# Low-part scores of a differential attention as two 64-row matmuls, both maps of a chunk together

## The chip, the cores and the metric

One NeuronCore of a Trainium2 chip runs the whole program. The metric is the device time of one execution in microseconds (us), the median of several runs; lower is better. TensorE is the matmul engine (PE in the profile, its weight loads PEld), VectorE is DVE, ScalarE is ACT, GpSimd is POOL, and SyncE (SP) issues DMAs.

## The reference, cut to what matters

One layer of an encoder over 2048 prompt frames and 64 sample frames. A combined input projection feeds two branches; the change is in the first, differential attention with 4 heads. Every head has two maps (m = 0, 1) with 64-wide queries and keys of their own, and one 128-wide value:

```python
scores = einsum('bqhmd,bkhmd->bhmqk', q, k) * ATTN_SCALE      # m = 0, 1; d = 64
scores = where(visible, scores + bias, -inf)                  # ALiBi, chunks of 64
p = softmax(scores)
a = p[:, :, 0] - lam * p[:, :, 1]
out = einsum('bhqk,bkhe->bqhe', a, v)
```

The second branch is a gated recurrence in chunks; both are normalised, gated and projected back.

## The kernel before

The program goes through the four heads one after the other (head 0 written out, heads 1 to 3 in a loop), and in each through 17 query tiles `t`: 16 prompt tiles of 128 frames and the sample tile (`SAMPLE`, 64 frames). A prompt tile `t` sees 128 (t + 1) keys, the sample tile 192; `chunks_of(t)` cuts the keys into chunks of up to 512, 41 chunks per head, of which 28 are 512 wide, four each 384, 256 and 128 wide, and one 192 (the sample's).

Matmuls here run on values split into a high part (type f32r) and a low part, the difference. For the scores the split is along the array's rows: for each map, 64 rows hold the high part of the keys and 64 the low part, `kp[:, m, :]`. The queries of a map come twice: `q2[:, m, 0, :]` has the high part in both halves of the rows, `q2[:, m, 1, :]` the low part in both. So two 128-row matmuls per map and chunk, which add up in one PSUM bank (`qkb[:, u % 2]`), make high times (high + low) and low times (high + low): line 660. Map 0 uses bank 0, map 1 bank 1.

TensorE's program for tile `t` is `project(h, t, first)`: two halves, b = 1 (the recurrence's columns) and then b = 0 (the attention's), each of 8 steps `kt` of three 512-column matmuls (line 534: high x with high and low weights, low x with high weights). The scores of the tile before are laid between these steps: the units (chunk, map), in order, one behind each of the steps kt = 1 to 7 of b = 1 and one behind kt = 0 of b = 0 (lines 542 to 546). Ahead of kt = 2 of b = 0 come the recurrence's scores of the tile before (`rec_scores`, line 560, same two banks), ahead of kt = 6 three transposes. Behind the projection come `rec_output` (lines 575 to 577), `attend` (transposes of the attention weights, line 596, and their products with the values, line 605) and the transposes of this tile's queries and keys (`transpose_qk`, lines 636 to 646). In the sample tile the line 605 and line 577 matmuls have 64 rows in one block each; float32 matmuls show as two instructions.

`qk(h, t, c, m)` waits for its bank (`qk_free`, signalled by VectorE's read two uses ago), issues its two matmuls and signals `qk_done`. VectorE's `biased_scores` (line 1055) reads each bank, adds the bias, keeps the running maximum and frees the bank, in the order chunk 0 map 0, chunk 0 map 1, chunk 1 map 0, and so on; between chunk 0 and 1 it does `finish` of the tile before, behind chunk 1 `apply_decay`. Then ScalarE takes the exponentials (line 828), and VectorE combines the maps (line 1077).

The natural-order copies of queries and keys are made by ScalarE (high parts, lines 773 and 774) and VectorE (low parts, lines 1003 and 1004) in `qn`, and transposed by TensorE into `q2` and `kp`. Behind the last head an epilogue projects back (lines 687 to 700).

Of the kernel before, what the change touches and what calls it, by code (L numbers as in the profile page):

```python
# [25 lines left out]
P = 128  # L26
# [5 lines left out]
HD = 64  # L32
VD = 128
CHUNK = 64
KT = D_MODEL // P
PT = SEQ // P
NT = PT + 1
SAMPLE = NT - 1
# [25 lines left out]
def chunks_of(t):  # L64
    k0, n = keys_of(t)
    return [(k0 + c, min(512, n - c), c) for c in range(0, n, 512)]
# [26 lines left out]
def build(nc, x_prompt, x_sample, cache_k, cache_v, state_h, norm_g, w_in, lambda_qk, subln_g, rec_lb,  # L93
# [5 lines left out]
    with ctx:  # L99
        def sb(name, shape, dt=f32):  # L100
            return ctx.enter_context(nc.sbuf_tensor(name, shape, dt))
# [13 lines left out]
        kp = sb("kp", [P, 2, SLOTS * P], f32r)  # L115
# [2 lines left out]
        bias = sb("bias", [P, SEQ])  # L118
        at = sb("at", [P, 2, 512])
        qn = sb("qn", [P, 8, P], f32r)  # L120
        q2 = sb("q2", [P, 2, 2, P], f32r)
        kn = sb("kn", [P, 2, P])
        zz = sb("zz", [P, 2, P])
# [100 lines left out]
        def need(eng, h, name, n):  # L224

            eng.wait_ge(S[name], h * PER[name] + (PRIME.get(name, 0) + n))
# [261 lines left out]
        def _(pe):  # L488
# [19 lines left out]
            def project(h, t, first):  # L508

                units = qk_units(t - 1) if t > 0 else []
                slot = t % XRING
                if first:
                    pe.wait_ge(S["x_hi"], t + 1)
                    pe.wait_ge(S["x_lo"], t + 1)
                else:
                    pe.wait_ge(S[f"xr_in{slot}"], (h - 1) * (16 * XR_PER[slot]) + 16 * (t // XRING + 1))
                steps = [(b, kt) for b in (1, 0) for kt in range(KT)]
                for b, kt in steps:  # L520
                    if kt == 0:
                        need(pe, h, ("qk_split", "pb_free")[b], t)
                    if b == 0 and kt == 6:
                        transpose_recurrence(h, t, first)
                    if b == 0 and kt == 2 and t > 0:
                        rec_scores(h, t - 1)
                    if t == 0 and b == 1:
                        name, n = lo_of(kt)
                        need(pe, h, "w_hi_ready", kt + 1)
                        need(pe, h, name, n)  # L530
                    for part in range(2):
                        x = xr[:, slot, part, kt, :]
                        for w in ((w_hi, w_lo) if part == 0 else (w_hi,)):
                            last = mm(pab[:, b, :], x, w[:, kt, 512 * b:512 * b + 512],  # L534
                                      start=(kt == 0 and part == 0 and w is w_hi),
                                      stop=(kt == KT - 1 and part == 1))
                    if t == SAMPLE and b == 0 and kt < KT - 1:
                        last.then_inc(S["w_freed"], 1)
                    if b == 1 and kt >= 1:
                        if first and kt == (2 if t > 0 else KT - 1) and t < NT - 1:  # L540
                            x_transposes(t + 1)
                        for c, m in units[kt - 1:kt]:
                            qk(h, t - 1, c, m)
                    if b == 0 and kt == 0:
                        for c, m in units[KT - 1:]:
                            qk(h, t - 1, c, m)
                    if kt == KT - 1:
                        last.then_inc(S[("proj_done", "proj_b")[b]], 1)

# [30 lines left out]
            def attend(h, t, first):  # L580
                if t == SAMPLE:
                    need(pe, h, "cache_in", 48)
                need(pe, h, "fin_done", t)
                chunks = chunks_of(t)

                if first and t + 2 < NT:
                    pe.wait_ge(S["x_lo"], t + 3)

                def transposes(c):
                    u = t_use["at", t, c]  # L590
                    need(pe, h, "t_evac", u - 1)
                    apart(pe)
                    need(pe, h, "combined", at_index[t, c] + 1)
                    apart(pe)
                    for b, _, n in blocks_of(t, c):
                        last = tr(tb[0:n, u % 2, b:b + P], scores[:, 0, chunks[c][2] + b:chunks[c][2] + b + n],  # L596
                                  ident[:, :])
                    last.then_inc(S["at_t"], 1)

                def values(c):  # L600
                    u = t_use["at", t, c]
                    need(pe, h, "t_evac", u + 1)
                    blocks = blocks_of(t, c)
                    for j, (b, slot, n) in enumerate(blocks):
                        last = mm(oar[:, 0, 0:VD], at[0:n, u % 2, b:b + P], vv[0:n, slot, :],  # L605
                                  start=(c == 0 and j == 0), stop=(c == len(chunks) - 1 and j == len(blocks) - 1))
                    return last

                transposes(0)
                for c in range(len(chunks)):  # L610
                    if t == SAMPLE - 1 and c == 1:
                        transpose_qk(h, SAMPLE)
                    if c + 1 < len(chunks):
                        transposes(c + 1)
                    last = values(c)
                    if t == SAMPLE - 1 and c == 1:
                        for m in range(2):
                            qk(h, SAMPLE, 0, m)
                last.then_inc(S["pv_done"], 1)

            def transpose_recurrence(h, t, first):
# [24 lines left out]
                        last = tr(tb[:, u % 2, P * j:P * j + P], qn[:, 4 + j, :].bitcast(f32), ident[:, :])  # L646
                last.then_inc(S["k_t"], 1)

            def qk_units(t):
                return [(c, m) for c in range(len(chunks_of(t))) for m in range(2)]  # L650

            def qk(h, t, c, m):

                if c == 0:
                    need(pe, h, "t_evac", t_use["k", t] + 1)
                k0, w, _ = chunks_of(t)[c]
                u = qk_use["qk", t, c, m]
                need(pe, h, "qk_free", u - 1)
                for part in range(2):
                    last = mm(qkb[:, u % 2, 0:w], q2[:, m, part, :], kp[:, m, k0:k0 + w],  # L660
                              start=(part == 0), stop=(part == 1))
                last.then_inc(S["qk_done"], 1)

            def head(h, first):
                for t in range(NT):
# [54 lines left out]
        def _(act):  # L720
# [47 lines left out]
            def attention_columns(h, t):  # L768
                need(act, h, "proj_done", t + 1)
                pa = pab[:, 0, :]  # L770
                q_out = qn[:, 0:4, :].rearrange("p (m a) (d e) -> p m a d e", m=2, d=2)[:, :, 0]
                q_in = pa[:, 0:P].rearrange("p (m e) -> p m e", m=2).unsqueeze(2).to_broadcast([P, 2, 2, HD])
                F(q_out, q_in, ACT.Copy)
                F(qn[:, 4:6, 0:HD], pa[:, P:2 * P].rearrange("p (m e) -> p m e", m=2), ACT.Copy)
                need(act, h, f"k_out{t % 2}", 16 * (t // 2))
                F(kn[:, t % 2, :], pa[:, P:2 * P], ACT.Copy)
                if t == 0:
                    need(act, h, "v_out", 0)
                F(vv[:, slot_of(t), :], pa[:, 2 * P:3 * P], ACT.Copy)
                F(zz[:, 0, :], pa[:, 3 * P:4 * P], ACT.Copy)  # L780
                F(ez[:, 0, :], pa[:, 3 * P:4 * P], ACT.Exp, scale=-1.0).then_inc(S["a_evac"], 1)
# [122 lines left out]
        def _(dve):  # L904
# [58 lines left out]
            def link(h, ins):  # L963

                chain[0] += 1
                ins.then_inc(S["vec_chain"], 1)
                need(dve, h, "vec_chain", chain[0])
# [30 lines left out]
            def attention_columns(h, t):  # L998
                need(dve, h, "a_evac", t + 1)
                pa = pab[:, 0, :]  # L1000
                q_blocks = qn[:, 0:4, :].rearrange("p (m a) (d e) -> p m a d e", m=2, d=2)
                q_in = pa[:, 0:P].rearrange("p (m e) -> p m e", m=2).unsqueeze(2).to_broadcast([P, 2, 2, HD])
                tt(q_blocks[:, :, 1], q_in, q_blocks[:, :, 0].bitcast(f32), ALU.subtract)
                tt(qn[:, 4:6, HD:P], pa[:, P:2 * P].rearrange("p (m e) -> p m e", m=2),
                   qn[:, 4:6, 0:HD].bitcast(f32), ALU.subtract).then_inc(S["qk_split"], 1)
                if t == SAMPLE:
                    need(dve, h, "cache_in", 48)
                    k_in = kc[:, :].rearrange("p (m e) -> p m e", m=2)
                    link(h, v.tensor_copy(qn[:, 6:8, 0:HD], k_in))
                    tt(qn[:, 6:8, HD:P], k_in, qn[:, 6:8, 0:HD].bitcast(f32), ALU.subtract  # L1010
                       ).then_inc(S["cache_split"], 1)

            def recurrence_columns(h, t):
# [292 lines left out]
```

## Time and profile before

| | |
|---|---|
| median of 3 runs | 1666.36 us (1665.0 to 1667.35) |
| span of the profiled execution | 1667.4 us |
| TensorE busy, matmuls | 1560.9 us (94%) |
| TensorE busy, weight loads | 1319.2 us (79%) |
| VectorE busy | 1184.7 us (71%) |
| ScalarE busy | 742.4 us (45%) |
| GpSimd busy | 656.1 us (39%) |
| granted TensorE clock, mean | 0.977 of full speed |

The durations of matmuls overlap: what a matmul costs in a stream is read from the distance of starts in the timeline, not from its own duration. "Idle before" says how long an engine stood before a group and what released it; "issue" means that the profile shows nothing that it waited for. A granted clock of 1.00 is 2.4 GHz, one of 0.50 is 1.2 GHz.

### The profile page before, as it was taken

The numbers are of one execution on the slowest core, as the hardware profiler recorded it, in microseconds if no ns is written. First come the engines' busy times: TensorE is split into PE (matmuls) and PEld (weight loads), VectorE is DVE, ScalarE is ACT, GpSimd is POOL, SyncE is SP. The second block draws the span as 40 slices with busy tenths as digits, with TensorE's granted clock in tenths as the row PEclk, the third lists the DMA queues.
The fourth block names the chain that finished last, engine by engine and source line by source line (L and its number), as shares of the span: only waits on it lengthen the run. The fifth ranks groups of instructions, "written<-read, shape, count | busy, mean of one in ns | idle before, by whom it ended". The sixth has DMA issues, their size and how long they took to land.

```text
span 1667.4 us, 28103 instructions
## 1 busy us (share of the span) xinstructions
PE 1560.9 (94%) x8576; PEld 1319.2 (79%) x8576; DVE 1184.7 (71%) x2410; ACT 742.4 (45%) x2009; POOL 656.1 (39%) x1392
## 2 busy tenths in 40 slices
PE   5999999997999999969999999969999999799998
PEld 4788888876888888857888888758888888588886
DVE  5888888786777777775777777867777777822322
ACT  4455555554444444453444444634444445511111
POOL 4654444424554444434544444334544444300000
PEclk9999999998999999989999999979999999899999
DMA  7232222143422111132322121143121110244341
GB/s 220 82 127 92 89 89 80 54 136 119 118 69 88 64 64 64 43 111 65 117 71 86 64 64 51 48 121 115 67 91 65 64 64 13 88 139 151 119 145 63
DMA packets 96200, 149.19 MB, mean 89 GB/s; under 512 B 7536, under 2 KB 77552, under 8 KB 87344
## 3 DMA queue, kind: packets, MB, share of 16 engines
q1 hardware_dynamic: 96048, 147.36, 27.2%
q8 instruction: 72, 1.18, 0.3%
q14 instruction: 80, 0.66, 0.1%
HBM read 102.76 MB, written 44.56 MB: 88 GB/s over the span
## 4 chain that ended last, share of the span: by engine, by line
PE 79%; DVE 8%; ACT 5%; issue 4%; DMA 2%; POOL 1%; SPq 1%; ACTq 0%; DVEq 0%; POOLq 0%
PE pab L534 40%; PE qkb L660 8%; PE oar L605 8%; PE pab L700 6%; PE qkb L700 5%; PE qkb L560 4%; PE tb L596 2%; PE tb L636 2%; DVE rc L1017 1%; ACT at L798 1%; DMA w_raw<-in_w_in 1%; DVE w_lo L931 1%; PE tb L687 1%; DVE scores L1077 1%; DVE st L995 1%
## 5 line engine op out<-in xcount | busy, mean ns | idle before, releaser
L534 PE MATMUL pab<-w_hi,xr 128*128 128x512 f32 x2176 | 791.5, 406 | 15.1 <-issue 9.0
L534 PEld LDWEIGHTS pab<-w_hi,xr 128*128 128x128 f32 x2176 | 415.4, 191 | 99.0 <-issue 18.7
L534 PE MATMUL pab<-w_lo,xr 128*128 128x512 f32 x1088 | 430.5, 396 | 0.0
L1249 POOL TENSOR_TENSOR dd<-dd 128x64 f32<-128x64 f32 x340 | 110.9, 326 | 614.2 <-DVE dd L1038 614.2
L534 PEld LDWEIGHTS pab<-w_lo,xr 128*128 128x128 f32 x1088 | 208.9, 192 | 32.9
L1055 DVE CUSTOM_DVE_ANT_0 scores<-qkb,bias 128x512 f32<-128x512 f32 (+4 forms) x136 | 84.6, 624 | 184.9 <-PE qkb L660 184.7
L605 PE MATMUL oar<-vv,at 128*128 128x128 f32 x1104 | 153.6, 285 | 34.0 <-ACT at L798 33.5
L660 PE MATMUL qkb<-kp,q 128*128 128x512 f32 (+3 forms) x656 | 184.2, 363 | 0.0
L786 ACT ACTIVATE fb<-pab 128x256 f32<-128x256 f32 x68 | 26.1, 384 | 350.5 <-PE pab L534 350.5
L605 PEld LDWEIGHTS oar<-vv,at 128*128 128x128 f32 x1104 | 134.5, 193 | 53.4 <-ACT at L798 52.5
L828 ACT ACTIVATE scores<-scores,nmx 128x128 f32<-128x128 f32 (+16 forms) x136 | 157.0, 1166 | 25.8 <-DVE nmx L1065 25.4
L1228 POOL TENSOR_TENSOR kq<-qt,xx 128x896 f32<-128x896 f32 x68 | 144.5, 2125 | 24.9 <-ACT xx L837 24.5
L660 PEld LDWEIGHTS qkb<-kp,q 128*128 128x128 f32 x656 | 120.4, 189 | 28.9 <-DVE mxs L1055 4.7
L1055 DVE CUSTOM_DVE_ANT_0 scores<-qkb,bias,mxs 128x512 f32<-128x512 f32 (+2 forms) x192 | 121.8, 646 | 20.4 <-PE qkb L660 9.8
L1174 POOL TENSOR_SCALAR tms<-tsq 128x1 f32<-128x1 f32 x34 | 6.5, 191 | 294.7 <-ACT at L891 106.5
L1023 DVE RECIPROCAL ez<-ez 128x256 f32<-128x256 f32 x68 | 119.2, 1753 | 2.3
L1017 DVE RECIPROCAL rc<-rc 128x256 f32<-128x256 f32 x68 | 119.2, 1753 | 2.3
L1250 POOL TENSOR_TENSOR dd<-dd 128x64 f32<-128x64 f32 x340 | 108.8, 320 | 0.0
L560 PEld LDWEIGHTS qkb<-kq 128*128 128x128 f32 x816 | 101.4, 191 | 7.3 <-DVE kq L1084 1.1
L995 DVE TENSOR_REDUCE st<-masked 128x128 f32<-128x768 f32 x68 | 103.6, 1523 | 2.3
L798 ACT ACTIVATE at<-tb 128x512 f32<-128x512 f32 (+3 forms) x164 | 84.8, 538 | 42.4 <-PE tb L596 40.5
L560 PE MATMUL qkb<-kq 128*128 128x128 f32 x816 | 102.7, 275 | 0.8 <-DVE kq L1084 0.4
(146 smaller groups left out, 2705.5 us busy)
## 6 DMA issues: line engine op xcount, KB each, us to landing
xr<-xs SPq DMA_DIRECT2D x51, 1024.0 KB, 5.3
xs<-xr SPq DMA_DIRECT2D x17, 1024.0 KB, 3.9
w_raw<-in_w_in SPq DMA_DIRECT2D x24, 512.0 KB, 6.6
mix<-mx SPq DMA_DIRECT2D x68, 128.0 KB, 2.2
bias<-mix SPq DMA_DIRECT2D x17, 512.0 KB, 5.4
w_raw<-in_x_prompt SPq DMA_DIRECT2D x16, 512.0 KB, 3.9
scores<-in_x_prompt SPq DMA_DIRECT2D x16, 512.0 KB, 4.8
out<-vv SPq DMA_DIRECT2D x16, 512.0 KB, 3.0
```

Of the source, the lines that this page charges most:

```text
L534: last = mm(pab[:, b, :], x, w[:, kt, 512 * b:512 * b + 512], start=(kt == 0 and part == 0 and w is w_hi), stop=(kt == KT - 1 and part == 1))
L560: last = mm(qkb[:, u % 2, P * j:P * j + P], kl[:, b, :], ql[:, q, :], start=True, stop=True)
L605: last = mm(oar[:, 0, 0:VD], at[0:n, u % 2, b:b + P], vv[0:n, slot, :], start=(c == 0 and j == 0), stop=(c == len(chunks) - 1 and j == len ...
L660: last = mm(qkb[:, u % 2, 0:w], q2[:, m, part, :], kp[:, m, k0:k0 + w], start=(part == 0), stop=(part == 1))
L700: last = mm(bank[:, b, :], x, w[:, kt, 512 * b:512 * b + 512], start=(kt == 0 and part == 0 and w is w_hi), stop=(kt == KT - 1 and part == 1))
L828: last = F(scores[:, m, 0:n], scores[:, m, 0:n], ACT.Exp, bias=nmx[:, m:m + 1], scale=SCALE, accum_out=sums[:, m:m + 1])
L995: v.tensor_reduce(st[:, :], masked[:, :, :].rearrange("p l c -> p c l"), AX.X, ALU.add).then_inc(S["rec_acc"], 1)
L1017: link(h, v.reciprocal(rc[:, :, :], rc[:, :, :]))
L1023: v.reciprocal(ez[:, :, :], ez[:, :, :]).then_inc(S["z_ready"], 1)
L1055: v.tensor_tensor_reduce(out=scores[:, m, off:off + w], in0=qkb[:, u % 2, 0:w], in1=bias[:, zero + off:zero + off + w], scale=1.0, scalar= ...
L1228: g.tensor_tensor(ql[:, :, :], qt[:, :].unsqueeze(1).to_broadcast([P, NS, P]), xx[:, NX - NS:NX, :], ALU.mult).then_inc(S["q_decayed"], 1)
L1249: g.tensor_tensor(o[:, :, 0, :], ref, c[:, :, 0, :], sub)
```

## The change

The keys' natural-order blocks are filled so that map 0 has its high part in the first 64 positions and its low part in the last 64, as before, and map 1 the other way round (`key_hi`, `key_lo`). So after the transposes `kp` holds the high keys of map 0 in rows 0 to 63 and those of map 1 in rows 64 to 127. The high part of the queries is multiplied as before, by one 128-row matmul per map. The low part of the queries is multiplied by the high keys alone, by one 64-row matmul per map: map 0 on rows 0 to 63, map 1 on rows 64 to 127. The product of low queries and low keys is left out.

A unit is now a whole chunk. `qk(h, t, c)` issues the high matmuls of both maps, each behind its bank's wait, and then the two low ones, each of which signals `qk_done`. Up to four chunks stand behind the steps kt = 1, 3, 5 and 7 of b = 1; nothing of it is left in b = 0.

```diff
+        def key_hi(block):
+            return qn[:, block:block + 2, :].rearrange("p b (d e) -> p (b d) e", d=2)[:, 0:4:3, :]
+        def key_lo(block):
+            return qn[:, block:block + 2, :].rearrange("p b (d e) -> p (b d) e", d=2)[:, 1:3, :]
...
-                units = qk_units(t - 1) if t > 0 else []
+                units = range(len(chunks_of(t - 1))) if t > 0 else []
...
-                        for c, m in units[kt - 1:kt]:
-                            qk(h, t - 1, c, m)
-                    if b == 0 and kt == 0:
-                        for c, m in units[KT - 1:]:
-                            qk(h, t - 1, c, m)
+                        if kt % 2 == 1:
+                            for c in units[kt // 2:kt // 2 + 1]:
+                                qk(h, t - 1, c)
...
-                        for m in range(2):
-                            qk(h, SAMPLE, 0, m)
+                        qk(h, SAMPLE, 0)
...
-            def qk(h, t, c, m):
+            def qk(h, t, c):
...
-                u = qk_use["qk", t, c, m]
-                need(pe, h, "qk_free", u - 1)
-                for part in range(2):
-                    last = mm(qkb[:, u % 2, 0:w], q2[:, m, part, :], kp[:, m, k0:k0 + w],
-                              start=(part == 0), stop=(part == 1))
-                last.then_inc(S["qk_done"], 1)
+                for m in range(2):
+                    u = qk_use["qk", t, c, m]
+                    need(pe, h, "qk_free", u - 1)
+                    mm(qkb[:, u % 2, 0:w], q2[:, m, 0, :], kp[:, m, k0:k0 + w], start=True, stop=False)
+                for m in range(2):
+                    u = qk_use["qk", t, c, m]
+                    rows = slice(HD * m, HD * m + HD)
+                    mm(qkb[:, u % 2, 0:w], q2[rows, m, 1, :], kp[rows, m, k0:k0 + w], start=False, stop=True
+                       ).then_inc(S["qk_done"], 1)
...
-                F(qn[:, 4:6, 0:HD], pa[:, P:2 * P].rearrange("p (m e) -> p m e", m=2), ACT.Copy)
+                F(key_hi(4), pa[:, P:2 * P].rearrange("p (m e) -> p m e", m=2), ACT.Copy)
...
-                tt(qn[:, 4:6, HD:P], pa[:, P:2 * P].rearrange("p (m e) -> p m e", m=2),
-                   qn[:, 4:6, 0:HD].bitcast(f32), ALU.subtract).then_inc(S["qk_split"], 1)
+                tt(key_lo(4), pa[:, P:2 * P].rearrange("p (m e) -> p m e", m=2),
+                   key_hi(4).bitcast(f32), ALU.subtract).then_inc(S["qk_split"], 1)
```

The cached keys of the sample tile are split in the same way (`key_hi(6)`, `key_lo(6)`).

## Rows read from the trace of the kernel before

**Rows 1.** The page: busy time by engine, and the last chain by line.
```profile
PE 1560.9 (94%) x8576; PEld 1319.2 (79%) x8576; DVE 1184.7 (71%) x2410; ACT 742.4 (45%) x2009; POOL 656.1 (39%) x1392
...
PE pab L534 40%; PE qkb L660 8%; PE oar L605 8%; PE pab L700 6%; PE qkb L700 5%; PE qkb L560 4%; PE tb L596 2%; PE tb L636 2%; DVE rc L1017 1%; ACT at L798 1%; DMA w_raw<-in_w_in 1%; DVE w_lo L931 1%; PE tb L687 1%; DVE scores L1077 1%; DVE st L995 1%
```

**Rows 2.** Waits of the span: engine line <- releaser: us in total, times, longest.
```profile
DVE scores L1055 <- PE qkb L660: 194.5, 153, 3.8
...
PE oar L605 <- ACT at L798: 33.5, 56, 3.0
```

**Rows 3.** Groups of TensorE by form (columns as the page's part 5).
```profile
L660 PE MATMUL qkb<-kp,q 128*128 128x512 f32 x448 | 140.0, 394 | 0.0
...
L660 PE MATMUL qkb<-kp,q 128*128 128x384 f32 x64 | 16.9, 345 | 0.0
```

**Rows 4.** Timeline of TensorE: start us, us, engine line op out<-in; 512-column matmuls.
```profile
1061.38 0.39 PE L534 MATMUL pab<-w_hi,xr 128*128 128x512 f32 x1
1061.61 0.62 PE L660 MATMUL qkb<-kp,q 128*128 128x512 f32 x2
1062.06 0.39 PE L534 MATMUL pab<-w_hi,xr 128*128 128x512 f32 x1
```

**Rows 5.** Timeline of TensorE: 256 columns at 782, 128 columns at 1020.
```profile
782.49 0.40 PE L660 MATMUL qkb<-kp,q 128*128 128x256 f32 x2
782.73 0.40 PE L534 MATMUL pab<-w_hi,xr 128*128 128x512 f32 x1
...
1020.49 1.50 PE L560 MATMUL qkb<-kq 128*128 128x128 f32 x12
1021.83 0.27 PE L564 MATMUL oar<-ident,kq 128*128 128x128 f32 x1
```

**Rows 6.** Timeline of TensorE, sample step of head 0, single matmuls.
```profile
391.64 0.42 PE L577 MATMUL oar<-vr,kd 64*128 64x128 f32 x1
391.99 0.79 PE L534 MATMUL pab<-w_hi,xr 128*128 128x512 f32 x1
392.58 0.63 PE L534 MATMUL pab<-w_lo,xr 128*128 128x512 f32 x1
```

**Rows 7.** Timeline of the weight loads (PEld) in the same place.
```profile
389.39 0.50 PEld L605 LDWEIGHTS oar<-vv,at 64*128 64x128 f32 x2 [0.22 <-issue]
...
390.50 0.55 PEld L576 LDWEIGHTS oar<-state_s,kq 128*128 128x128 f32 x2
391.27 0.50 PEld L577 LDWEIGHTS oar<-vr,kd 64*128 64x128 f32 x2 [0.23 <-issue]
391.99 0.29 PEld L534 LDWEIGHTS pab<-w_hi,xr 128*128 128x128 f32 x1 [0.22 <-issue]
```

**Rows 8.** Loads and matmuls where TensorE restarts at full clock.
```profile
1065.05 0.30 PEld L660 LDWEIGHTS qkb<-kp,q 128*128 128x128 f32 x2 [0.31 <-DVE mxs L1055]
...
1065.05 0.73 PE L660 MATMUL qkb<-kp,q 128*128 128x512 f32 x2
1065.62 0.39 PE L534 MATMUL pab<-w_hi,xr 128*128 128x512 f32 x1
```

**Rows 9.** Ends of score matmuls and reads by VectorE, at 948 and 1065.
```profile
948.15 0.62 PE L660 MATMUL qkb<-kp,q 128*128 128x512 f32 x2
...
948.96 0.69 DVE L1055 CUSTOM_DVE_ANT_0 scores<-qkb,bias 128x512 f32<-128x512 f32 x1 [0.45 <-PE qkb L660]
...
1064.25 0.74 DVE L1055 CUSTOM_DVE_ANT_0 scores<-qkb,bias,mxs 128x512 f32<-128x512 f32 x1
1064.92 0.08 DVE L1055 DVE_READ_ACCUMULATOR2_ANT mxs<- 128x1 f32 x1
...
1066.06 0.75 DVE L1055 CUSTOM_DVE_ANT_0 scores<-qkb,bias,mxs 128x512 f32<-128x512 f32 x1 [0.39 <-PE qkb L660]
```

**Rows 10.** Stretches: us, busy us (x) of each engine, granted clock, DMA share, GB/s.
```profile
388.60:391.90 3.30, 3.23 (x10) 2.42 (x10) 2.26 (x3) 2.13 (x3) 1.70 (x1) 0.50 1.06 360
1060.00:1067.00 7.00, 7.00 (x31) 5.55 (x30) 6.07 (x17) 0.89 (x4) 2.56 (x3) 1.00 0.44 154
```

More of the change, by code:

```diff
@@ L647, in transpose_qk @@
                 last.then_inc(S["k_t"], 1)
-            def qk_units(t):
-                return [(c, m) for c in range(len(chunks_of(t))) for m in range(2)]
-            def qk(h, t, c, m):
+            def qk(h, t, c):
                 if c == 0:
@@ L1008, in attention_columns @@
                     k_in = kc[:, :].rearrange("p (m e) -> p m e", m=2)
-                    link(h, v.tensor_copy(qn[:, 6:8, 0:HD], k_in))
-                    tt(qn[:, 6:8, HD:P], k_in, qn[:, 6:8, 0:HD].bitcast(f32), ALU.subtract
+                    link(h, v.tensor_copy(key_hi(6), k_in))
+                    tt(key_lo(6), k_in, key_hi(6).bitcast(f32), ALU.subtract
                        ).then_inc(S["cache_split"], 1)
```

## The prediction, made before the changed kernel ran

> **What bounds the kernel now.** I read the page first: TensorE is busy for 94% of the span, and the chain that ended last runs over it for 79%, 8% of it at the score matmuls of line 660 [rows 1]. The list of waits says how little TensorE stands still: its longest total is 33.5 us behind ScalarE's copies of the attention weights, while VectorE waits 194.5 us for the scores themselves [rows 2]. So a VectorE delay of some tenths of a microsecond is covered wherever VectorE stands waiting, and a tenth that TensorE gains or loses inside the projection is worth a tenth of the total. The groups by form give what the change touches: 656 score matmuls, 448 of them 512 columns wide, 64 of 384, and as many of 256 and of 128; the remaining 16 are the sample's, 192 wide [rows 1, 3]. Four belong to a chunk (two maps, high and low part): 112 + 16 + 16 + 16 + 4 = 164 chunks.
>
> The timeline of TensorE gives the price of one. From 1061.38 to 1062.06 three 512-column matmuls of two kinds start, so 0.227 us each, back to back; the recorded 0.39 us is latency, not cost [rows 4]. At 256 columns two take 0.24 us, 0.12 each, and twelve 128-column matmuls take 1.34 us, 0.112 each [rows 5]. Streaming at the granted 2.4 GHz takes 512/2.4 = 0.213, 0.160 for 384, 0.107 for 256, 0.053 for 128; for 384 I take a spacing of 0.175, for 192 the 0.12 of 256. At 128 columns the spacing is no longer the stream's: it is that of the weight loads, about 0.11 us each.
>
> **What goes.** If the two 64-row matmuls of a chunk run at once on the two halves of the rows, a chunk costs three matmuls and not four. The second can't start before its own weights are in, one load (0.107) after the first. It then costs 0.107 where a full spacing stood: minus 0.12 for 112 chunks, minus 0.07 for 16, about nothing for the rest: 13.4 + 1.1 + 0.4 = 15 us gained. That is all the pairing can bring if loads follow each other; if the second load is hidden too, the whole spacing goes: 112 x 0.227 + 16 x 0.175 + 16 x 0.12 + 16 x 0.112 + 4 x 0.12 = 32 us.
>
> The Trainium skill (TensorE: Matmul & The Clock Gate, Part 3) says that matmuls on different row groups start about 4 ns apart. By that the pair would cost nothing beyond one matmul; no trace row has two row groups side by side. This is the source beside the fast rival below.
>
> **What comes: two changes between 128-row and 64-row matmuls per chunk.** The kernel before has 64-row matmuls in one place, the sample step of every head (16 of them), and there the trace shows what they do to their neighbours. The weight loads of TensorE normally run ahead: from line 575 to 576 (both 128 rows) there is no gap. Into line 577 (64 rows) the load stands idle 0.23 us "on issue", and out of it, into line 534 (128 rows), 0.22 us again [rows 7]. Between two matmuls of one line 605 loop, where the code has no wait at all, the same 0.22 stands at the step to 64 rows [rows 7]; all four heads repeat the pattern. I take that as a cost of the change of rows: the next weights aren't loaded until the matmul before is through.
>
> The size: the second matmul of line 577 starts at 391.64, and the next load, of line 534, at 391.99, 0.35 later [rows 6]. This stretch has a granted clock of 0.50, so 1.2 GHz, and the score stretches have 1.00 [rows 10]. At 1.2 GHz 128 columns stream for 0.107, so 0.245 us pass between the end of the stream and the load. Then the load itself is exposed: the second matmul of line 534 starts at 392.58, one cold stream (0.427) behind the first, which so began at 392.15, 0.16 after its load.
>
> At full clock both have to be scaled. The exposed load has a warm row: at 1065.05 TensorE restarts after a bank wait, and the third matmul from there starts 0.57 later where two spacings are 0.455, so an exposed load costs 0.115 [rows 8]. The gap has no warm row. Recorded latency beyond the stream is 0.42 - 0.107 = 0.31 for that cold matmul [rows 6] and 0.39 - 0.213 = 0.18 for a warm one [rows 4]; the gap is 0.07 shorter than the cold one, so about 0.11 warm; half of 0.245 is 0.12. I take 0.12, with zero and the unscaled 0.245 as ends. A negative cost is excluded: waiting for a drain can't start the next matmul sooner.
>
> The Trainium skill (TensorEngine Tiling (Array Packing), Key Properties) says that changing the tiling mode, not just the tile, drains TensorE. It speaks against this change and names no clock at which the drain would vanish; by it the fast rival would be out, and the sum below stands.
>
> One change of rows at 512 columns so costs 0.213 + 0.12 + 0.115 = 0.448 from start to start in place of 0.227: 0.22 more. At 384 it is 0.22, at 256 0.22, at 128 0.176 and at 192 0.195 more (0.08 + 0.235 against 0.12). Two per chunk, and the pair's second start:
> - 512: 0.44 + 0.107 - 0.227 = 0.32, times 112 = 35.8
> - 384: 0.44 + 0.107 - 0.175 = 0.37, times 16 = 6.0
> - 256: 0.44 + 0.107 - 0.12 = 0.43, times 16 = 6.9
> - 128: 0.35 + 0.107 - 0.112 = 0.345, times 16 = 5.5
> - 192: 0.39 + 0.107 - 0.12 = 0.38, times 4 = 1.5
>
> Sum: 55.7 us, all on TensorE's own path.
>
> **What moves.** Map 1's scores are issued one projection step (three matmuls, 0.68) earlier, and both maps of a chunk now follow each other. Each waits for VectorE to have read its bank. Behind such a wait stand map 1's matmul, the low pair and the rest of the projection. From the start of the last low matmul: its end is recorded 0.39 later. VectorE starts 0.28 behind an end (1065.78 to 1066.06), takes 0.67 per read and 0.08 for the accumulator (1064.25, 1064.92), and TensorE restarts 0.05 after that, at 1065.05 [rows 8, 9]. VectorE's first read hangs on the first low matmul, 0.107 earlier, so bank 1 is free at -0.107 + 0.39 + 0.28 + 1.34 + 0.08 + 0.05 = 2.03. TensorE asks for it at 0.448 + six spacings (1.36) + one (0.227) = 2.04. So no wait in the forecast, by a hair: the drains pay for it. Without the drains TensorE asks at 1.81 and waits 0.22. That holds behind a second or third chunk (12 per head, 48). Behind the first chunk (as many) VectorE starts only 0.19 after the end (948.77 to 948.96) and a read is 0.05 shorter, 0.69 against 0.74, so 0.19 of it goes and 0.03 is left. That would be 48 x 0.25 = 12 us. What VectorE does after chunk 0 and chunk 1 (finish, apply_decay) fits into a spacing of 2.6 per chunk.
>
> **Costed at nothing:** the keys' split on ScalarE and VectorE writes as many elements in another order, and both engines have idle time (busy for 45% and 71% of the span [rows 1]). Waits, semaphore signals and matmuls per chunk are as many as before. The low part no longer adds low queries times low keys, which was in the same matmul and cost no time. The sample's chunk sits between transposes and value matmuls and has the same two changes.
>
> **The sum.** The profiled execution spans 1667.4 us, 1 above the median of the runs (1666.36). 1667.4 + 55.7 = 1723.1, so 1722 for the median.
>
> **The rivals.**
> - *The change of rows costs nothing at full clock, and the second load is hidden too (faster).* For it: all 64-row rows lie at half clock, behind idle time. Against it: the gap is at each of the changes, and nowhere between equal rows. Price: -32, and bank waits of 0.33 and 0.14 (the first read no longer starts early) give back 48 x 0.47 = 22: -10, 1656, between 1634 and 1663. It decides when a change costs under about 0.06 to 0.11 us at 512 columns; I have 0.22.
> - *No cost of the change, loads in a row:* -15 + 12 = -3, so 1664, no difference that can be told.
> - *Only the load is exposed, no gap:* 0.213 + 0.115 - 0.227 = 0.10 per change. 112 x 0.08 + 16 x (0.13 + 0.19 + 0.11) + 0.4 = 16, and bank waits of 0.11 at 48 places, 5: 1687.
> - *Gap not scaled (0.245), or the pair one after the other:* the first adds 328 x 0.125 = 41 us, 1763; the second 112 x 0.12 + 16 x 0.07 = 15, 1737. Both 1778.
>
> **How the numbers follow.** Gap scaled, pair overlapping, 1700 to 1745: 0.55. Dearer, 1737 to 1778: 0.15. Load only, 1672 to 1700: 0.11. No cost and no gain, 1663 to 1670: 0.06. Faster, 1634 to 1663: 0.13. A measurement tells about 0.2% (3.3 us) from no change. Slower is 0.55 + 0.15 + 0.11 = 0.81. The range 1668 to 1765 leaves out the fast case, most of the neutral one and the top.
>
> **What would show it.** In the timeline of TensorE after: two score matmuls of 128 rows 0.227 apart; the load of the first 64-row one some 0.33 behind the second's start, idle on "issue"; the second 64-row matmul 0.11 behind the first (overlap) or 0.23 (none); the next projection matmul 0.45 behind that. TensorE's idle time should grow, not its matmul time alone, and bank waits stay small. I am wrong if the loads of the 64-row matmuls start while the matmul before still streams, or if the waits grow behind VectorE's reads.

## The result and the profile after

The changed kernel takes 1703.1 us (median of four), against 1666.9 for the kernel before in the same runs: 1.0215 times as long, 95% interval 1.0197 to 1.0234. One of the four executions took 3915.7 us, for a reason that no trace here shows, and counts only in that median; the other three took 1698.7, 1702.3 and 1703.9 us, and the ratio is from them. In a second set of runs it took 1700.9 against 1665.7, 1.0204 (1.0187 to 1.0221). So 35 to 36 us slower. The profiled execution spans 1697.0 us, 29.6 more than that of before; its own time, 1698.7, lies 4 us below that median.

The page of the changed kernel, busy time, granted clock and last chain by line:

```profile
PE 1594.6 (94%) x8576; PEld 1284.9 (76%) x8576; DVE 1186.0 (70%) x2410; ACT 739.8 (44%) x2009; POOL 653.9 (39%) x1392
...
PEclk9999999998999999989999999989999999899999
...
PE pab L541 41%; PE oar L610 8%; PE pab L704 6%; PE qkb L704 5%; PE qkb L565 5%; PE qkb L661 4%; PE qkb L665 4%; PE tb L640 2%; ACT at L802 1%; DVE scores L1059 1%; PE tb L601 1%; DMA w_raw<-in_w_in 1%; DVE w_lo L935 1%; PE tb L691 1%; ACT qn L778 1%
```

Against [rows 1] TensorE's matmul time has gone up by 33.7 us, though a quarter of the score matmuls (the second of each low pair) now stream beside another one. The granted clock is about the same, 0.981 on average against 0.977. Line 660 was 8% of the chain; lines 661 (high part) and 665 (low part) are 4% each, so the chain spends about as long on the scores as before.

The groups by form, TensorE (busy us, mean ns of one | idle before), 512 columns:

```profile
L661 PE MATMUL qkb<-kp,q 128*128 128x512 f32 x224 | 75.0, 406 | 0.1
...
L665 PE MATMUL qkb<-kp,q 64*128 64x512 f32 x224 | 56.1, 497 | 0.0
```

The low matmuls last 497 ns each, but 224 of them are busy for only 56.1 us. That is 112 times 0.50: the two of a chunk lie on top of each other. By the single records of the trace the second of a pair starts 3 ns behind the first (median of all 164 pairs; 2 to 5 ns), and so do their weight loads. Compare [rows 3], 448 matmuls of 394 ns.

The timeline of TensorE in one chunk of 512 columns, and then its weight loads there:

```profile
1031.36 0.64 PE L661 MATMUL qkb<-kp,q 128*128 128x512 f32 x2
1031.93 0.50 PE L665 MATMUL qkb<-kp,q 64*128 64x512 f32 x2
1032.35 0.50 PE L541 MATMUL pab<-w_hi,xr 128*128 128x512 f32 x1
1032.69 0.40 PE L541 MATMUL pab<-w_lo,xr 128*128 128x512 f32 x1
```

```profile
1031.15 0.40 PEld L661 LDWEIGHTS qkb<-kp,q 128*128 128x128 f32 x2
1031.93 0.19 PEld L665 LDWEIGHTS qkb<-kp,q 64*128 64x128 f32 x2 [0.37 <-issue]
1032.35 0.19 PEld L541 LDWEIGHTS pab<-w_hi,xr 128*128 128x128 f32 x1 [0.24 <-issue]
```

The weight load of the low pair (x2: both loads, 0.19 us together) stands idle "on issue" and begins at 1031.93; the next load of the projection again stands idle and begins 0.42 later. The list of waits further down has 135 such waits of the projection's loads, where the kernel before had 11. From the first high matmul (1031.36) to where the projection goes on is 1.10 us: the second projection matmul starts at 1032.69, so the first, one spacing before it, at 1032.46. Four spacings of 0.227 would be 0.91. (A matmul whose load was exposed is recorded here from the start of that load, so the pair streams from about 1032.04, 0.11 behind 1031.93.)

A third difference is in the next views: TensorE's matmuls and loads at the second and third chunk of this tile, and VectorE's reads between them:

```profile
1033.85 0.63 PE L661 MATMUL qkb<-kp,q 128*128 128x512 f32 x2
1034.41 0.49 PE L665 MATMUL qkb<-kp,q 64*128 64x512 f32 x2
...
1036.34 0.82 PE L661 MATMUL qkb<-kp,q 128*128 128x512 f32 x2
```

```profile
1033.97 0.19 PEld L661 LDWEIGHTS qkb<-kp,q 128*128 128x128 f32 x1 [0.17 <-DVE mxs L1059]
...
1036.12 0.19 PEld L661 LDWEIGHTS qkb<-kp,q 128*128 128x128 f32 x1
1036.66 0.19 PEld L661 LDWEIGHTS qkb<-kp,q 128*128 128x128 f32 x1 [0.35 <-DVE mxs L1059]
1037.09 0.19 PEld L665 LDWEIGHTS qkb<-kp,q 64*128 64x128 f32 x2 [0.24 <-issue]
```

```profile
1035.18 0.75 DVE L1059 CUSTOM_DVE_ANT_0 scores<-qkb,bias,mxs 128x512 f32<-128x512 f32 x1 [0.48 <-PE qkb L665]
1035.86 0.08 DVE L1059 DVE_READ_ACCUMULATOR2_ANT mxs<- 128x1 f32 x1
1035.86 0.75 DVE L1059 CUSTOM_DVE_ANT_0 scores<-qkb,bias,mxs 128x512 f32<-128x512 f32 x1
1036.53 0.08 DVE L1059 DVE_READ_ACCUMULATOR2_ANT mxs<- 128x1 f32 x1
```

The load for the second map's high matmul comes at 1036.66, 0.05 behind VectorE's release of the bank at 1036.61 (1036.53 + 0.08). With the load at 1036.66 the matmul starts at about 1036.77, where one spacing behind the first (1036.34) would have been 1036.57: 0.2 us of bank wait. At the second chunk the load is listed as idle for 0.17 too, but it lost nothing: the pair follows 0.56 behind the first high matmul (1033.85 to 1034.41), as in the first chunk (0.57). So the list counts idle time of the loads, and only part of it is time lost. The waits of the weight loads in the whole span (us in total, times, longest):

```profile
PEld pab L541 <- issue: 38.1, 135, 2.8
PEld qkb L665 <- issue: 37.7, 128, 0.4
PEld qkb L661 <- DVE mxs L1059: 21.7, 72, 0.5
```

In the kernel before, the first and the last of them were:

```profile
PEld pab L534 <- issue: 18.7, 11, 3.9
...
PEld qkb L660 <- DVE mxs L1055: 4.7, 16, 0.3
```

### The profile page after: what moved, and what is told of

Same layout as the page of the kernel before. It is cut to its first block, busy times and chain, and to the rows that moved or that the text cites. A ratio compares the mean times of both kernels' runs of the same rounds, so it can differ in the third digit from the quotient of the medians.

```text
span 1697.0 us, 28086 instructions
## 1 busy us (share of the span) xinstructions
PE 1594.6 (94%) x8576; PEld 1284.9 (76%) x8576; DVE 1186.0 (70%) x2410; ACT 739.8 (44%) x2009; POOL 653.9 (39%) x1392
## 4 chain that ended last, share of the span: by engine, by line
PE 80%; DVE 8%; ACT 6%; issue 3%; DMA 2%; SPq 1%; POOL 0%; DVEq 0%; ACTq 0%; POOLq 0%
PE pab L541 41%; PE oar L610 8%; PE pab L704 6%; PE qkb L704 5%; PE qkb L565 5%; PE qkb L661 4%; PE qkb L665 4%; PE tb L640 2%; ACT at L802 1%; DVE scores L1059 1%; PE tb L601 1%; DMA w_raw<-in_w_in 1%; DVE w_lo L935 1%; PE tb L691 1%; ACT qn L778 1%
## 5 line engine op out<-in xcount | busy, mean ns | idle before, releaser
L541 PE MATMUL pab<-w_hi,xr 128*128 128x512 f32 x2176 | 783.6, 413 | 11.1 <-DVE w_lo L935 7.6
L1059 DVE CUSTOM_DVE_ANT_0 scores<-qkb,bias 128x512 f32<-128x512 f32 (+4 forms) x136 | 80.0, 622 | 169.4 <-PE qkb L665 169.1
L1059 DVE CUSTOM_DVE_ANT_0 scores<-qkb,bias,mxs 128x512 f32<-128x512 f32 (+2 forms) x192 | 118.4, 649 | 50.4 <-PE qkb L665 48.8
L661 PE MATMUL qkb<-kp,q 128*128 128x512 f32 (+4 forms) x328 | 103.5, 377 | 1.5 <-DVE mxs L1059 0.2
L1081 DVE SCALAR_TENSOR_TENSOR scores<-scores,cneg 128x512 f32<-128x512 f32 (+4 forms) x164 | 100.6, 662 | 2.4
```

What stands on the lines that cost most here:

```text
L661: mm(qkb[:, u % 2, 0:w], q2[:, m, 0, :], kp[:, m, k0:k0 + w], start=True, stop=False)
L1059: v.tensor_tensor_reduce(out=scores[:, m, off:off + w], in0=qkb[:, u % 2, 0:w], in1=bias[:, zero + off:zero + off + w], scale=1.0, scalar= ...
```

## The experiments

Theory A: each change between 128-row and 64-row matmuls costs TensorE about 0.2 us, the pair overlaps, and the rest is small. Rival B: grouping the maps and waiting for banks is what costs. Rival C: the pair doesn't overlap. Rival D: 64-row matmuls are dear in themselves.

**full_rows: the change without its 64 rows.**

```diff
-                    rows = slice(HD * m, HD * m + HD)
-                    mm(qkb[:, u % 2, 0:w], q2[rows, m, 1, :], kp[rows, m, k0:k0 + w], start=False, stop=True
+                    mm(qkb[:, u % 2, 0:w], q2[:, m, 1, :], kp[:, m, k0:k0 + w], start=False, stop=True
                        ).then_inc(S["qk_done"], 1)
```

> The change's order and key layout, but the low matmuls over all 128 rows again, so no change between 64 and 128 rows and four full matmuls per chunk. Theory A (the change of rows costs about 0.2 us each way, the grouping little): back near the kernel before, 1667 to 1673 us, with bank waits of about 0.1 us behind some chunks. Rival B (issuing both maps together and waiting for VectorE's banks is what costs): it stays near the changed kernel, 1695 to 1705 us.

Measured: 1668.3 us, 1.0005 of before (0.9992 to 1.0019). The loads' bank waits are there:

```profile
PEld qkb L661 <- DVE mxs L1058: 22.5, 81, 0.5
```

They are as many as in the changed kernel, and yet the total is that of before. So the key layout, the new order and the grouping together cost nothing that can be measured; B falls as the main cause. The 35 us come with the 64-row matmuls. The two traces place them: from the first high matmul of a 512-column chunk to the second projection matmul behind it, the changed kernel takes 0.17 us longer than full_rows, on average as in the median of the 112 chunks. Two changes at 0.20 less one spacing are 0.17.

**same_rows: the pair on the same rows.**

```diff
-            return qn[:, block:block + 2, :].rearrange("p b (d e) -> p (b d) e", d=2)[:, 0:4:3, :]
+            return qn[:, block:block + 2, 0:HD]
...
-            return qn[:, block:block + 2, :].rearrange("p b (d e) -> p (b d) e", d=2)[:, 1:3, :]
+            return qn[:, block:block + 2, HD:P]
...
-                    rows = slice(HD * m, HD * m + HD)
+                    rows = slice(0, HD)
```

> The change's order, but with the keys laid out as before, so that both 64-row low matmuls use rows 0 to 63 and can't run at once. Theory A (in the changed kernel the pair overlaps wholly, two changes of rows per chunk): one full spacing per chunk comes on top, +32 us, and the bank waits of about 13 us go, since TensorE comes later: 1717 to 1728 us. Rival C (the two low matmuls of the changed kernel run one after the other anyway): no difference, 1700 to 1706 us.

Measured: 1719.2 us, 1.0312 of before (1.0281 to 1.0343), 16 to 18 more than the changed kernel. Its group of low matmuls at 512 columns, and a chunk in the timeline:

```profile
L665 PE MATMUL qkb<-kp,q 64*128 64x512 f32 x224 | 81.7, 444 | 0.0
```

```profile
1022.27 0.61 PE L661 MATMUL qkb<-kp,q 128*128 128x512 f32 x2
1022.82 0.73 PE L665 MATMUL qkb<-kp,q 64*128 64x512 f32 x2
1023.48 0.50 PE L541 MATMUL pab<-w_hi,xr 128*128 128x512 f32 x1
1023.81 0.40 PE L541 MATMUL pab<-w_lo,xr 128*128 128x512 f32 x1
```

Now 224 low matmuls are busy for 81.7 us, not 56.1. The pair's load to the projection's next load takes 0.66 (1022.82 to 1023.48), where it was 0.42: one spacing more. So in the changed kernel the pair does run at once; C falls. The total grew by less than 32 us. That fits the bank waits, which fall from 21.7 us to 1.5 in the list; the expectation had put 13 us on them.

**pair_twice: the low pair issued twice (the low part is added twice).**

```diff
+                for again in range(2):
...
+                        last = mm(qkb[:, u % 2, 0:w], q2[rows, m, 1, :], kp[rows, m, k0:k0 + w],
+                                  start=False, stop=(again == 1))
+                        if again == 1:
+                            last.then_inc(S["qk_done"], 1)
```

> The changed kernel with its low pair issued twice in a row (so the low part is added twice); two 64-row matmuls more per chunk, no change of rows more. Theory A (the cost sits at the changes, the pair overlaps): one spacing per chunk more (112 x 0.227 + 16 x 0.175 + 16 x 0.12 + 16 x 0.112 + 4 x 0.12 = 32 us), 1732 to 1738 us. Rival C (the pair runs one after the other): two spacings, 1763 to 1770 us. Rival D (every 64-row matmul is dear, not the change): the extra pair costs as much as the first with its changes, about 0.63 us per chunk, 1800 us.

Measured: 1732.8 us, beside 1700.9 for the changed kernel in the same runs: 31.9 us more, where 32 was worked out. Two more 64-row matmuls per chunk cost exactly one spacing:

```profile
1028.24 0.61 PE L661 MATMUL qkb<-kp,q 128*128 128x512 f32 x2
1028.78 0.73 PE L666 MATMUL qkb<-kp,q 64*128 64x512 f32 x4
1029.44 0.50 PE L541 MATMUL pab<-w_hi,xr 128*128 128x512 f32 x1
1029.78 0.39 PE L541 MATMUL pab<-w_lo,xr 128*128 128x512 f32 x1
```

Load to load 0.66 us again, for four matmuls and not two; the listed bank waits (22.5 us) are those of the changed kernel. D falls: what costs is going to 64 rows and back, not being there.

**units_64: the kernel before, with the low matmul of every unit on 64 rows.**

```diff
                 for part in range(2):
-                    last = mm(qkb[:, u % 2, 0:w], q2[:, m, part, :], kp[:, m, k0:k0 + w],
+                    rows = (slice(0, P), slice(0, HD))[part]
+                    last = mm(qkb[:, u % 2, 0:w], q2[rows, m, part, :], kp[rows, m, k0:k0 + w],
```

> The order and placement of the kernel before (a unit is one map of a chunk, keys laid out as before); only the low matmul of each unit takes 64 rows (rows 0 to 63, low queries times high keys). So as many matmuls of the same width as before and four changes of rows per chunk in place of none. Theory A: each change costs 0.205 at 512 columns, 0.20 at 384, 256 and 192, 0.156 at 128: 4 x (112 x 0.205 + 36 x 0.20 + 16 x 0.156) = 131 us on top of the kernel before, 1785 to 1800 us. Rival B (grouping and bank waits are what costs): 1665 to 1670 us.

Measured: 1786.4 us, 1.0723 of before (1.0705 to 1.0741), 120.7 us more, for as many matmuls of the same widths and 656 changes of rows: 0.184 us each over all widths. A unit of 512 columns in the timeline, and the waits of the loads in the span:

```profile
1020.87 0.82 PE L661 MATMUL qkb<-kp,q 128*128 128x512 f32 x2
1021.62 0.50 PE L534 MATMUL pab<-w_hi,xr 128*128 128x512 f32 x1
1021.95 0.39 PE L534 MATMUL pab<-w_lo,xr 128*128 128x512 f32 x1
```

```profile
PEld qkb L661 <- issue: 100.6, 318, 0.4
PEld pab L534 <- issue: 81.2, 267, 4.4
```

The unit takes 0.85 us (1020.87 to 1021.95 - 0.23 = 1021.72) in place of two spacings, 0.454: 0.20 for each of its two changes. This is the cleanest price, since TensorE has no wait behind `mxs`, so no bank wait, in this kernel's list. It is 10 us below the expectation's 131. In the traces, from a unit's first matmul to the second projection matmul behind it (medians against the kernel before), a change costs 0.20 at 512 columns, 0.19 at 384 and 256, and 0.14 at 128 and 0.17 at 192; the expectation had 0.205, 0.20, 0.20, 0.156 and 0.20. That accounts for about 4 of the 10 us, and the rest stays open.

**one_low and one_low_early: three full matmuls per chunk.** Both leave out the low part of map 0. In one_low both maps are handed to VectorE at the end of the last matmul; in one_low_early map 0 at the end of its own.

```diff
-                    mm(qkb[:, u % 2, 0:w], q2[:, m, 0, :], kp[:, m, k0:k0 + w], start=True, stop=False)
-                for m in range(2):
-                    u = qk_use["qk", t, c, m]
-                    rows = slice(HD * m, HD * m + HD)
-                    mm(qkb[:, u % 2, 0:w], q2[rows, m, 1, :], kp[rows, m, k0:k0 + w], start=False, stop=True
-                       ).then_inc(S["qk_done"], 1)
+                    mm(qkb[:, u % 2, 0:w], q2[:, m, 0, :], kp[:, m, k0:k0 + w], start=True, stop=(m == 0))
+                mm(qkb[:, u % 2, 0:w], q2[:, 1, 1, :], kp[:, 1, k0:k0 + w], start=False, stop=True
+                   ).then_inc(S["qk_done"], 2)
```

one_low_early signals 1 behind `m == 0` and 1 at the end.

> Leaves out the low part of map 0; map 1's low part is one 128-row matmul, and both maps are handed to VectorE at its end. So three full matmuls per chunk, as much streaming as the changed kernel, without a change of rows. Theory A: 32 us less matmul time than before, some 22 us of bank waits back: 1650 to 1662 us. Rival B (grouping and bank waits cost): 1690 us or more. What it is below the changed kernel is the price of the changes of rows.

> As one_low (the low part of map 0 is left out), but map 0 is handed to VectorE at the end of its own high matmul, two matmuls earlier. Theory A with the bank waits as worked out (bank 1 free 1.69 us behind the last matmul, asked for at 1.81): no bank waits, 1632 to 1642 us, about 20 us below one_low. If the bank waits are not set by when VectorE starts on map 0, it is the same as one_low.

Measured: 1661.3 us, 0.9960 (0.9948 to 0.9972), and 1631.1 us, 0.9781 (0.9752 to 0.9811). A chunk of one_low and one of one_low_early:

```profile
1034.51 0.39 PE L661 MATMUL qkb<-kp,q 128*128 128x512 f32 x1
1035.07 0.50 PE L661 MATMUL qkb<-kp,q 128*128 128x512 f32 x1 [0.17 <-DVE mxs L1056]
1035.41 0.39 PE L662 MATMUL qkb<-kp,q 128*128 128x512 f32 x1
1035.64 0.40 PE L541 MATMUL pab<-w_hi,xr 128*128 128x512 f32 x1
```

```profile
1031.88 0.62 PE L661 MATMUL qkb<-kp,q 128*128 128x512 f32 x2
1032.33 0.39 PE L664 MATMUL qkb<-kp,q 128*128 128x512 f32 x1
1032.56 0.39 PE L541 MATMUL pab<-w_hi,xr 128*128 128x512 f32 x1
```

In one_low the second high matmul waits for its bank: its load begins at 1035.07, so it streams from about 1035.18, 0.44 later than one spacing behind the first. In one_low_early it follows at once: 0.45 for two, then 0.23. The bank waits of the loads in the whole span, one_low and then one_low_early:

```profile
PEld qkb L661 <- DVE mxs L1056: 38.4, 86, 0.6
```

```profile
PEld qkb L661 <- DVE mxs L1058: 12.4, 35, 0.5
```

The same matmuls, and 30 us between them, 26 of them in this list. The expectation had 20 us and no bank waits at all in one_low_early; it came out 1 us below its range, with a third of the waits left. With no change of rows in the way, most of the gain of a matmul saved can be lost to when VectorE may begin: one_low kept 6 of 32 us. That is the sum of the prediction's fast rival (32 us gained, 22 given back, 1656 us) seen on the chip, with 26 us given back.

**early_64: one_low_early with its low matmul on 64 rows.**

```diff
-                mm(qkb[:, u % 2, 0:w], q2[:, 1, 1, :], kp[:, 1, k0:k0 + w], start=False, stop=True
+                mm(qkb[:, u % 2, 0:w], q2[HD:P, 1, 1, :], kp[HD:P, 1, k0:k0 + w], start=False, stop=True
```

> one_low_early (the low part of map 0 left out, map 0 handed over early) with its one remaining low matmul on 64 rows in place of 128: nothing but the rows of 164 matmuls differs, and VectorE's reads lie where the bank waits are few. Theory A: two changes of rows per chunk, 2 x (112 x 0.205 + 36 x 0.20 + 16 x 0.156) = 65 us on top of the 1631 us of one_low_early, less a few us of bank waits: 1688 to 1698 us. If much of what was put down to the changes were bank waits in the runs before, it stays below 1675 us.

Measured: 1681.2 us, 1.0089 of before (1.0069 to 1.0109): 50 us above one_low_early, below the expected 57 to 67. (The two ran in different sets; against the kernel before of each set the step is 52 us.) A chunk:

```profile
1023.69 0.61 PE L661 MATMUL qkb<-kp,q 128*128 128x512 f32 x2
1024.24 0.49 PE L664 MATMUL qkb<-kp,q 64*128 64x512 f32 x1
1024.66 0.50 PE L541 MATMUL pab<-w_hi,xr 128*128 128x512 f32 x1
1025.00 0.40 PE L541 MATMUL pab<-w_lo,xr 128*128 128x512 f32 x1
```

From 1023.69 to 1024.77 (1025.00 - 0.23) is 1.08 us, where three spacings are 0.68: again 0.20 per change in place. Over the kernel it is 50/328 = 0.15, net of what is given back elsewhere: one_low_early's remaining bank waits, 12.4 us in the list above, are gone in this kernel's list, where TensorE comes later. They and the lower price at narrow chunks are about the missing 15 us; how they divide was not measured.

**spread: chunks three steps apart in tiles with up to three.**

```diff
-                        if kt % 2 == 1:
-                            for c in units[kt // 2:kt // 2 + 1]:
+                        step = 3 if len(units) < 4 else 2
+                        if kt % step == 1:
+                            for c in units[kt // step:kt // step + 1]:
```

> The changed kernel, but in tiles with up to three chunks these stand three projection steps apart (behind kt = 1, 4, 7) and not two. Theory A with bank waits of about 0.11 us per two-chunk tile and 0.38 per three-chunk tile in the changed kernel: these go, 4 x (4 x 0.11 + 4 x 0.38) = 8 us, so 1693 to 1698 us. Rival E (the bank waits are hidden elsewhere, or the later scores hold up the softmax): 1702 us or more.

Measured: 1700.9 us, 1.0202 of before (1.0185 to 1.0219), the same as the changed kernel beside it (1700.9). The bank waits did fall from 21.7 us to:

```profile
PEld qkb L662 <- DVE mxs L1060: 12.8, 41, 0.4
```

Yet the total doesn't move. The distances between the starts of the projection's matmuls, beside those of changed_again, say where it goes, in the 16 tiles that issue three chunks. Up to the end of the b = 1 half they are 7 us shorter together (0.4 to 0.6 us each in heads 1 to 3), so the waits did go. Their b = 0 halves are 2 us longer, and behind their projections 4 us are lost, 3.4 of them in head 0. The expectation (1693 to 1698) missed. Bank waits in these tiles were mostly given back, and why is not shown.

**changed_again** is the changed kernel beside the last ones.

> The changed kernel itself, beside the runs of this call: 1700 to 1706 us by either theory.

Measured: 1700.9 us, 1.0204 of before, as given above.

## Why the prediction was right in direction and large by half

Forecast 1722 (range 1668 to 1765), measured 1703 and 1701: +56 against +35 to +36. The sum was 70.6 us for 328 changes of rows, 17.5 for the pair's second start, minus 32.4 for the matmul saved, bank waits nothing.

- **The change of rows: right, at full clock too.** The row that carried the prediction was from 1.2 GHz and had to be scaled. Second high matmul (1031.59, one spacing behind the first) to the pair's load (1031.93): 0.34, forecast 0.333. One change so came to (1.10 - 0.23)/2 = 0.435 from start to start, forecast 0.448. Over the whole kernel units_64 gives 0.184 a change where the sum had 0.215: 60 us for 328, not 71. That term was 10 us too large.
- **The pair's second start: the step that failed.** I had it 0.107 behind the first, one weight load. The two loads are recorded together in 0.19 us, and the two matmuls lie on top of each other, 3 ns apart; same_rows and pair_twice say the same. The term is nil, 17.5 us too large, and without it my sum gives 38 us, or 1705. The row I took it from (128-column matmuls spaced by their loads, [rows 5]) holds for loads into the same rows and says nothing on two halves. The Trainium skill (TensorE: Matmul & The Clock Gate, Part 3) says that matmuls on different row groups start about 4 ns apart. The traces agree, with 3 ns.
- **The matmul saved: right.** pair_twice prices one spacing per chunk at 31.9 us, forecast 32.
- **No bank waits: wrong, for half by the same step.** The formula asked for the bank at 2.04 us and had it free at 2.03, with the first read 0.107 early because of the pair's late second start. With the pair at once the first read begins that much later. The other half is the exposed load: 2.03 is when the load may begin, 2.04 when the matmul was due, and the 0.115 between a load and its matmul, priced for the change of rows, was left out here. Both together are about the 0.2 us that the trace shows at the third chunk. In the sum over the kernel it is small: 60 - 32 = 28, measured 35 to 36, so 7 us for bank waits and all else, not separated; full_rows has the same listed waits and stands 0.8 us above the kernel before.
- **The signs.** The load of the pair came 0.34 behind the second high matmul (0.33 said) and the projection 0.42 behind the pair's streaming (0.45 said). Two signs came out otherwise. TensorE's idle time did not grow (1667.4 - 1560.9 = 106.5 us before, 102.4 after): the lost time stands in the longer records of the matmuls, 497 ns in place of 394, and the gap is seen only at the weight loads. And the waits behind VectorE's reads grew, from 4.7 to 21.7 us, which the prediction had named as a sign of being wrong; it was, in the term above.
- **How good the number is.** The errors partly cancel: 10 and 17.5 us too much, 7 too little, so 1722 in place of 1702. The range, 97 us wide, held rivals of other mechanisms too (load only, 1687); it is the traces, not the total, that tell them apart.
- **The gain of the pairing can't show by itself.** The fast rival (1656) assumed that changes cost nothing. They cost. But even free changes would have left little, as one_low shows: three full matmuls per chunk with late hand-over are 6 us faster than before, not 32. The rivals that put bank waits at 12 to 22 us without the changes had the right scale, if slightly low (26 in one_low).
- **Costed at nothing, and nothing:** key layout, order, grouping (full_rows, 1.0005).

Per 512-column chunk the change buys 0.227 us and pays about 0.41. By the prices of units_64 one pair of 64-row matmuls per two changes doesn't come out ahead at the narrower widths either: 0.38 paid for 0.175 bought at 384 columns, 0.39 for 0.12 at 256, 0.29 for 0.112 at 128. At 512 columns the two sides would meet where one pair of changes serves nearly two chunks (0.41/0.227 = 1.8), an estimate that wasn't tried.

## What to carry to other kernels

Before packing half-height matmuls side by side, count how often TensorE must go from full rows to half rows and back: here each change costs most of a 512-column matmul, and saving one matmul for every two changes loses. Look for a place in the old trace where the rows change already and read there how far the next load starts behind the matmul before it. Here that came out right from a stretch at half clock, once the part beyond the streaming was halved (0.12 forecast, 0.13 seen); that halving was a guess with two arguments behind it, and one case doesn't make it a rule. The idle time that the load is listed with (0.22 to 0.37) is not the price. Where a matmul group ends in a hand-over to the engine that frees its banks, hand each bank over as early as its own last matmul allows: the same three matmuls differed by 30 us in that alone.

## What the runs showed of the hardware that I had not expected

- Two 64-row matmuls on the two halves of the rows, in two PSUM banks, take the time of one, their weight loads too: 224 of 497 ns in 56.1 us busy, starts 3 ns apart.
- Going from 128 to 64 rows and back costs 0.20 us for each change beside 512-column matmuls at 2.4 GHz, whether the low matmul follows on the same bank (units_64, early_64) or on another one (changed kernel).
- The order of hand-over alone (one_low against one_low_early) was worth 30 us, 1.8% of the kernel.
